# A transformer layer with gathered experts on one core: attention of chunks 3 to 7 split in two stages by head group, expert rows fetched in pairs from pick 80

## What is computed

```python
h = x + W_out [ gnorm(MLA group) ; gnorm(dilated-window group) ]
h = h + MemoryCrossAttn(rmsnorm(h), rmsnorm(mem))
h = h + PEER(rmsnorm(h))
out = rmsnorm(h)

def chunk(xc):                        # PEER, 128 tokens at a time
    q = (xc @ w_q).reshape(C, Hh, 2, half)
    s = jnp.einsum('chpd,hpnd->chpn', q, sub_keys)
    top_s, top_i = lax.top_k(s, K)
    ...
    expert = ia * PEER_KEYS + ib
    g = jax.nn.softmax(best_s, axis=-1)
    u = u_tab[expert]
    a = jax.nn.gelu(jnp.einsum('cd,chkd->chk', xc, u), approximate=False)
    return jnp.einsum('chk,chkd->cd', g * a, v_tab[expert])
```

## Time and profile before

| | before |
|---|---|
| time of three runs | 3798.14, 3781.03, 3800.05 us (median 3798.14) |
| profiled execution | span 3789.9 us; its own time isn't given apart, the span lies between the three times |
| PE busy | 2933.6 us, 77% |
| DVE busy | 2484.4 us, 66% |
| ACT busy | 1298.0 us, 34% |
| POOL busy | 1420.4 us, 37% |
| DMA | 1297.10 MB, mean 342 GB/s |

### The profile page before, as it was taken

The page is one execution under the profiler, slowest core; times in us unless marked ns, Lnnn a source line. Parts: engine busy times, 40 slices in busy tenths (PEclk is TensorE's granted clock), DMA queues, the critical chain, the costliest instruction groups (busy, mean ns, idle before and its releaser), DMA issues.

```text
span 3789.9 us, 34958 instructions
## 1 busy us (share of the span) xinstructions
PE 2933.6 (77%) x8920; PEld 1517.5 (40%) x8920; DVE 2484.4 (66%) x5699; ACT 1298.0 (34%) x3333; POOL 1420.4 (37%) x1367
## 2 busy tenths in 40 slices
PE   8797866984886598989689797787878777766665
PEld 6655533431443355555344343333333333322222
DVE  0321218786876477767437888877887887788765
ACT  1212312221121244444234544444443454344333
POOL 0000003443776376657423333333333333333332
PEclk9897888997898799999899999999989999999999
DMA  7844156777998999999889999999999999999998
GB/s 298 274 147 184 57 215 214 238 263 283 346 338 327 352 369 341 363 352 355 333 318 369 401 411 417 409 414 415 411 407 421 413 405 407 421 410 414 417 411 351
DMA packets 274454, 1297.10 MB, mean 342 GB/s; under 512 B 27888, under 2 KB 63088, under 8 KB 180464
## 3 DMA queue, kind: packets, MB, share of 16 engines
q0 software_dynamic: 195120, 1073.83, 72.2%
q1 hardware_dynamic: 74384, 203.74, 14.4%
q10 hardware_dynamic: 4752, 17.30, 1.2%
HBM read 1231.07 MB, written 63.70 MB: 342 GB/s over the span
## 4 chain that ended last, share of the span: by engine, by line
DMA 31%; issue 7%; DVE 5%; PE 4%; ACT 3%; POOL 0%; POOLq 0%; DVEq 0%; SPq 0%; ACTq 0%
DMA s_ring<-peer_uv,s_expert 17%; DMA e_more_slots<-peer_uv,s_expert 10%; PE e_acc L503 3%; DVE e_part L427 1%; PE e_product L1859 1%; DMA e_more_slots<-peer_v,s_expert 1%; DMA next_h<-e_h 1%; DMA e_h<-norm_ffn_row 1%; DMA s_scratch<-norm_final_row 1%; DVE s_ring L394 1%; ACT L341 1%; ACT s_diagonal L324 0%; ACT s_gate L343 0%; DVE s_dots L394 0%; DVE e_more_slots L394 0%
## 5 line engine op out<-in xcount | busy, mean ns | idle before, releaser
L503 PE MATMUL e_acc<-s_ring,s_diagonal 128*128 128x512 f32 (+1 forms) x2168 | 898.8, 543 | 379.6 <-ACT s_diagonal L324 352.8
L394 DVE CUSTOM_DVE_ANT_0 s_ring<-s_ring,e_x_copy 128x1024 f32<-128x1024 f32 x548 | 666.6, 1217 | 221.9 <-DMA s_ring<-peer_uv,s_expert 215.1
L503 PEld LDWEIGHTS e_acc<-s_ring,s_diagonal 128*128 128x128 f32 x2168 | 396.5, 199 | 943.5 <-ACT s_diagonal L324 587.5
L278 POOL DMA_INDIRECT s_ring<-peer_uv,s_expert x462 | 437.5, 947 | 783.1 <-DVE e_part L427 551.8
L278 POOL DMA_INDIRECT s_ring<-peer_u,s_expert x331 | 377.4, 1140 | 449.9 <-DVE s_expert L1796 230.8
L503 PE MATMUL e_acc<-e_more_slots,s_diagonal 128*128 128x512 f32 (+1 forms) x948 | 387.4, 536 | 153.9 <-ACT s_diagonal L324 146.3
L278 POOL DMA_INDIRECT s_ring<-peer_v,s_expert x325 | 373.2, 1148 | 332.0 <-PE e_acc L503 94.9
L341 ACT ACTIVATE s_dots<-s_dots 128x1 f32<-128x1 f32 x704 | 142.2, 202 | 961.3 <-DVE s_dots L394 959.0
L324 ACT ACTIVATE s_diagonal<-s_ident,s_gate 128x128 f32<-128x128 f32 x949 | 371.2, 399 | 223.0 <-PE e_acc L503 100.1
L278 POOL DMA_INDIRECT e_more_slots<-peer_uv,s_expert x231 | 217.6, 942 | 413.8 <-DVE e_part L427 273.5
L394 DVE CUSTOM_DVE_ANT_0 s_ring<-s_ring,s_x 128x1024 f32<-128x1024 f32 x245 | 299.5, 1222 | 104.6 <-DMA s_ring<-peer_u,s_expert 69.2
(11 more groups left out here) (233 smaller groups left out, 3618.5 us busy)
## 6 DMA issues: line engine op xcount, KB each, us to landing
w_in_kept<-w_in SPq DMA_DIRECT2D x8, 1104.0 KB, 11.8
w_in_gained<-w_in_kept SPq DMA_DIRECT2D x8, 1104.0 KB, 10.2
p_w_in<-w_in_gained SPq DMA_DIRECT2D x8, 1104.0 KB, 19.0
f_w_big<-w_mem_kv SPq DMA_DIRECT2D x4, 2048.0 KB, 19.2
f_w_big<-peer_w_q_t SPq DMA_DIRECT2D x2, 4096.0 KB, 17.9
peer_scores<-f_stage_s SPq DMA_DIRECT2D x16, 512.0 KB, 8.5
e_mem_scores<-mem_scores SPq DMA_DIRECT2D x2, 4096.0 KB, 14.6
e_mem_values<-mem_values SPq DMA_DIRECT2D x2, 4096.0 KB, 25.0
```

The source lines that it names most:

```text
L278: pool.indirect_dma_start(out=to, out_offset=None, in_=table, in_offset=bass.IndirectOffsetOnAxis(ap=self.expert[c % PICK_BUFFERS][:, k:k ...
L394: dve.tensor_tensor_reduce(row, row, x[:, :], 1.0, 0.0, ALU.mult, ALU.add, self.dots[:, k:k + 1]).then_inc(self.u_used, 1)
L503: last = pe.matmul(self.acc[:, at:to], self.diagonal[:, made % DIAGONALS, :], row[:, at:to], start=(n == group[0]), stop=(n == group[-1]))
```

## The change

Six things change together.

1. `PAIRS_FROM` goes from 331 to 80. u and v of a pick are gathered in one transfer from row 160 on, and u no longer leads there. `ALONE_FROM` follows, 320 to 80: from pick 80, Gelu and product are made for each pick by itself (`coeff_alone` is now `make_coeffs`).
2. The attention of chunks 3 to 7 becomes two blocks, `attend_group` for the MLA heads (rows 304 to 448) and for the dilated heads (rows 448 to 640). Units run head by head, the five chunks of a head in turn. A bias table is loaded once a head. The normalized output of both groups stays in SBUF (`mixed`), and the five output projections come after the last unit of the second block, 16 of weight each beside nb + 3 for a unit.
3. Buffers that a block doesn't need go to the ring: 6, 10, 8 and 4 slots more than 8 in the four later stages (before: none, none, 4).
4. In the attention blocks PE takes 384 columns of v, before 512.
5. DVE adds a pick's v one pick later (`add_due`), in pairs' rows of the split stages too.
6. In `project_tokens` ACT takes the stream at two more places.

A stage can also be `batched`, Gelu for four picks at once; no stage here is.

```diff
-PAIRS_FROM = 331
+PAIRS_FROM = 80
...
-    def coeff_alone(self, g):
+    def make_coeffs(self, picks):
         act = self.nc.scalar
-        c, k = divmod(g, PICKS)
-        n = g - ALONE_FROM + 1
-        if k % (2 * TOPK) == 0 or n == 1:
+        c, k = divmod(picks[0], PICKS)
+        made = picks[0] - ALONE_FROM
+        many = len(picks)
+        if k % (2 * TOPK) == 0 or made == 0:
             act.wait_ge(self.gate_ready, GROUPS * c + k // (2 * TOPK) + 1)
-        act.wait_ge(self.u_used, g + 1)
...
+        act.wait_ge(self.u_used, picks[-1] + 1)
+        act.activation(self.active[:, k:k + many], self.dots[:, k:k + many], ACT.Gelu).then_inc(self.activated_alone, many)
+        act.wait_ge(self.activated_alone, made + many)
+        for g in picks:
+            at = g % PICKS
+            act.activation(self.coeff(g), self.active[:, at:at + 1], ACT.Copy, scale=self.coeff(g)).then_inc(self.coeff_made, 1)
+        act.wait_ge(self.coeff_made, made + many)
...
+        if self.batched[self.stage_of[n]]:
+            behind = {0: [n - 8, n - 6], 1: [n - 6, n - 4]}.get(g % BATCH, [])
+            last = [n - 6, n - 4, n - 2, n]
+        else:
+            behind = [n - 2]
+            last = [n]
+        for m in behind + (last if n == end - 1 else []):
+            if m >= first:
+                add(m)
...
+                if woven:
+                    beside(stream.scalar, t, 3)
+                if more:
                     keep_x_t(t + 1)
...
+def attend_group(nc, io, group, first, end, mixed, stream, until):
...
+        UNITS = [(h, t, first + t + 1) for h in range(HEADS) for t in range(COUNT)]
...
+        weights = np.array([nb + 3 for _, _, nb in UNITS] + ([FINISH_WEIGHT] * COUNT if group == 1 else []))
+        rows_until = [begin + int(c) for c in np.floor((until - begin) * np.cumsum(weights) / weights.sum())]
...
+            stream.scalar(begin)
+            softmax(0)
+            for n, (h, t, nb) in enumerate(UNITS):
+                act.wait_ge(p_turned, n + 1)
+                act.activation(probs_t[:, n % 2, 0:P * nb], turned[:, 0:P * nb], ACT.Copy).then_inc(p_t_ready, 1)
+                stream.scalar(rows_until[n])
+                if n < LAST:
+                    softmax(n + 1)
...
+            for n, (h, t, nb) in enumerate(UNITS):
+                pe.wait_ge(exped, n + 1)
+                for k in range(nb):
+                    last = pe.transpose(turned[:, P * k:P * (k + 1)], probs[:, n % 2, P * k:P * (k + 1)], ident[:, :])
+                last.then_inc(p_turned, 1)
+                if n + 2 <= LAST:
+                    score(n + 2)
+                weigh(n)
+                stream.tensor(rows_until[n])
...
-PICK_FIRST, PROJECT_REST, ATTEND_REST = 150, 300, 640
-STAGES = [(PICK_FIRST, "pe", D), (PROJECT_REST, "split", 0), (ATTEND_REST, "split", BANK), (len(ROWS), "pe", 3 * D // 4)]
+PICK_FIRST, PROJECT_REST, ATTEND_MLA, ATTEND_REST = 150, 304, 448, 640
+STAGES = [Stage(PICK_FIRST, "pe", D), Stage(PROJECT_REST, "split", 0, 6), Stage(ATTEND_MLA, "split", 3 * P, 10),
+          Stage(ATTEND_REST, "split", 3 * P, 8), Stage(len(ROWS), "pe", 3 * D // 4, 4)]
```

More of the change, by code:

```diff
@@ L215, in __init__, with batch_at, picks_due @@
             self.loads.append(used[slot])
+    def batch_at(self, n):
+        return next(batched for (start, until, _), batched in zip(self.stages, self.batched) if start <= n < until)
+    def picks_due(self, n):
+        g = ROWS[n][1]
+        if not self.batched[self.stage_of[n]]:
+            return [g]
+        return list(range(g + 1 - BATCH, g + 1)) if g % BATCH == BATCH - 1 else []
     def mode(self, n):
@@ L1154, in _, with attend @@
                 stream.tensor(until)
-def attend(nc, io, keep, first, end, ident=None, stream=None, until=0):
+def attend(nc, io, keep, first, end):
     with ExitStack() as ctx:
@@ L1195, in attend @@
         heads_out = ps("a_heads_out", [P, WIDTH])
-        if stream is not None:
-            stream.acc = ps("a_acc", [P, BANK])
-            start = stream.at["vector"]
-            weights = np.array([nb + 3 + (PROJECT_BLOCKS if i > 0 and u == PROJECT_AT else 0) for i, u, nb in ALL_UNITS])
-            HEAD_ROWS, TAIL = 8, 8
-            begin = start + HEAD_ROWS
-            rows_until = [begin + int(c) for c in np.floor((until - TAIL - begin) * np.cumsum(weights) / weights.sum())]
         w_loaded = sem("a_w_loaded")
@@ L1307, in _ @@
             act.wait_ge(eps_set, 1)
-            if stream is not None:
-                stream.scalar(begin)
             softmax(0)
@@ L1404, in _ @@
         def _(pool):
-            if stream is not None:
-                stream.gpsimd(stream.ahead(until))
-                return
             pool.wait_ge(gain_loaded, 16)
@@ L1440, in weigh @@
                 pe.wait_ge(p_t_ready, n + 1)
-                if stream is not None and n == 0:
-                    pe.wait_ge(keep_loaded["values"], 16)
                 if u in (0, HEADS):
@@ L1497, in _ @@
                     weigh(n)
-                    project(t - 1, (rows_until[n - 1], rows_until[n]) if stream is not None else (0, 0))
+                    project(t - 1)
                 if n + 2 < len(ALL_UNITS):
```

428 lines of the change are left out of this document (322 added, 106 removed).

## The result

The changed kernel takes 3955.40 us, median of four runs (3953.85 to 3960.31); the kernel before takes 3792.59 us beside it (3781.03 to 3800.05). The ratio is 1.0438, 95% interval 1.0415 to 1.0460: slower by 4.4%. The profiled execution took 3953.91 us with a span of 3952.1. I had said 3905, within 3815 to 3965, and slower with a chance of 0.80: the time lies in the range, 9.6 us from its upper end.

What follows compares the result with a forecast made beforehand. ACT's cycle in the attention units was taken as the bound (chance 0.78). Attention +108, projection +5 and last stage -3 gave +110 us: 3900 on the 3789.9 span, 3908 on the median; said 3905, range 3815 to 3965.

Steps and rivals of the forecast that it cites:

- Direction and mechanism: Attention units: ACT's cycle of copy, Gelu's table, picks, Exp's table and Exp sets the pace; slower, chance 0.80.
- The dearer switch: Rival for ACT's table switches: a drain makes each 2.66 us, not 1.30, an estimated 185 us more; chance 0.02.
- two starts: Start of each attention block, before its units run: 28 us each, 56 together, bounds 15 and 50 each.
- the units: 80 attention units, one head of one chunk each: 6.97 us in the first half, 7.12 in the second, 564 together.
- end of the first block: Ten norms and squares, a flush and a barrier closing the first attention half: 10 us.
- projections and tail: Five output projections alone behind the units, 100 us (bounds 90 and 110), and a tail of 8 us.
- idle while PE transposes: ACT's idle time in each attention unit: 0.74 us at 512 keys, 1.18 at 1024, mean 0.96.
- The second way: Cross-check of the attention: 264 us of added ACT work against 177 us of absorbable idle time, 87 more than fits.
- DMA's pace: Rival, projection and attention: ACT's slack suffices and wider gathers pay, up to 179 us faster; chance 0.12.
- Projection: Projection stage: ACT's late squares and roots cost 5.4 us a chunk, DVE's row waits go; +5 us, bounds -15 and +30.
- Last stage: Stage that ends the kernel: 22 single rows at its start become 11 pairs, same bytes to fetch; -3 us.

Runs made afterwards that it cites:

- e1: Changed kernel with one unused Sqrt, of another table, ahead of Exp in every attention unit: 4077.48 us, ratio 1.0731.
- e3: Changed kernel with Copy in place of Gelu in the two attention blocks, so nearly no table switches (output leaves out those Gelus): 3757.27 us, ratio 0.9881.
- e5: Changed kernel with one Gelu for four picks in the two attention blocks, pairs kept: 3843.16 us, ratio 1.0091.
- e9: Changed kernel with eight useless transposes of the identity added on PE in each attention unit: 3936.22 us, ratio 1.0384.
- e8: Changed kernel with the extra slots of the two attention blocks cut from 10 and 8 to 2 and 2: 3955.83 us, ratio 1.0376.
- e6: Changed kernel with the next unit's Exp (ACT) and transposes (PE) put ahead of the picks, all table loads kept in the code: 3863.07 us, ratio 1.0139.
- e2: Changed kernel with picks taken only in every second attention unit, twice as many at once: 3996.72 us, ratio 1.0521.
- e4: Changed kernel with double rows from pick 331 again, so one Gelu for 16 picks before; split attention and extra slots kept: 3794.65 us, ratio 0.9964.

## Why the prediction was right, and where it was off

*Direction and mechanism.* Right. Between two copies stand two table loads and the picks, with 1.18 us idle. Adding loads (e1) and taking them away (e3, e5) give nearly the same price: 111.2 us for 114.7 of added work, 1.25 us for each of 165, 1.30 us for each of 88. Each of these three has something else in it (the clock, the next bound, the shared Gelus), so the price is about the load's own length, and no closer than that.

*The dearer switch.* It did not come. The Trainium skill ("ScalarE: Activation LUTs", section "What ACT_TABLE_LOAD costs") has a drain of about 1380 ns beside each load. No trace here shows it: in the timeline above the load of 1297.72 ends at 1299.00 and Exp starts at 1299.02, e1 adds 77 loads and loses no more than the added work, and e3 gets 1.25 us back for each switch.

*The size.* I said +108 us for the attention, and it is +166.0. That the total is still inside my range is in part luck: the range had bounds for the starts, the projections and the projection stage and none for the unit, and the unit is where most of the difference lies. The terms against the copies' timeline of the changed kernel:

| term | said | measured | how |
|---|---|---|---|
| two starts | 56 | 71.2 | 36.9 (to 1271.44) and 34.3 (to 1609.56) |
| the units | 564 | 596.0 | 287.0 to the 40th copy at 1558.41, 309.0 to the one at 1918.57 |
| end of the first block | 10 | 16.9 | 1558.41 to 1575.3 |
| projections and tail | 108 | 111.7 | 1918.57 to 2030.3 |
| sum | 738 | 795.8 | |

The mis-sized term is the unit: 6.97 and 7.12 us from copy to copy, measured 7.36 and 7.92 (287.0 and 309.0 over 39 steps each; the last unit is in the row that follows). For the 78 steps that makes 46.5 us. The waits of ACT close this sum. It stood idle for the transposes for 107.0 us, where 0.96 a step makes 74.9: 32.1 us. It waited for dots for 8.5 us and for DVE at the end of a chunk for 3.5, which I had put at nothing: 12.0 us. Its own work, with the small gaps between instructions, is 2.4 us more than I had. So the step that was off is "idle while PE transposes", taken from two units in which PE was on time. Where PE was on time, as in the unit above (from the load at 1294.59 to the copy's end at 1302.46, 7.87 us at 1024 keys with two picks), it holds: 1.30 for the load, 1.84 for the picks, 1.30, Exp 1.15 less 0.10 of overlap, 0.19 for the read, 1.18 idle and 1.02 for the copy are 7.88. What the sum left out:

- **The clock.** I took PE's times from a stretch at 0.93. With PE waiting for Exp in most units, the blocks had 0.83. The unit ahead of the one shown took 9.31 us (copies at 1284.35 and 1293.66), with the same number of picks, 2:

```profile
1293.66 0.92 ACT L1647 ACTIVATE g_probs_t_g<-g_turned_g 128x896 f32<-128x896 f32 x1 [2.92 <-PE g_turned_g L1792]
```

and PE in it, against the same four matmuls of two picks a unit later:

```profile
1289.97 2.87 PE L560 MATMUL g_acc_g<-g_more_slots_g,s_diagonal 128*128 128x384 f32 x4
1292.64 0.98 PE L1792 MATMUL g_turned_g<-s_ident,g_probs_g 128*128 128x128 f32 x7
...
1296.90 0.91 PE L560 MATMUL g_acc_g<-g_more_slots_g,s_diagonal 128*128 128x384 f32 x2 [0.50 <-ACT s_diagonal L355]
1297.76 0.91 PE L560 MATMUL g_acc_g<-s_ring,s_diagonal 128*128 128x384 f32 x2
```

  2.87 us for four against 0.91 + 0.91. The granted clock was 0.50 from 1284 to 1290 and 0.66 from 1290 to 1294, and 1.00 in the 8 us behind. PE, late with the picks, came late to the transposes, and ACT waited 2.92 us for them, not 0.96. Sixteen of the 78 steps took over 8.5 us. e9, whose edit adds nothing but the filling on PE, got 23.1 us of the units back with the higher clock, and 24.9 us of waits for the transposes, where the excess of these was 32.1.

- **The end of a chunk of picks.** Its sums go out through DVE and ACT's own queue, and Exp stands behind them. It made the longest step of all, 15.18 us:

```profile
1737.58 1.28 ACT L373 ACT_TABLE_LOAD   x1 [3.54 <-DVE s_scratch L538]
...
1743.58 0.20 ACT L373 ACTIVATE s_dots<-s_dots 128x1 f32<-128x1 f32 x1 [3.75 <-DVE s_dots L428]
```

  That is some 7 us above the mean step; its two waits, 3.54 and 3.75 us, are part of the 12.0 us.

*The second way*, 264 us of work less 177 of slack, gave +87, with a second start some 115, and came no nearer: it took all of ACT's idle time but 77 us as free to use, and 155.4 us stayed idle ahead of the copies.

*Starts.* 35.6 us each in place of 28, within my bounds; PE waits for the block's own q for 24.3 and 20.3 us in the waits above. Most of the difference is the wide prefetch beside these first loads: with 2 slots more than 8 (e8) they are 30.6 and 26.8 us.

*DMA's pace.* I gave 0.12 to a gain of up to 179 us. Without Gelu's switches (e3) the pairs bring 25.3 us at most. My bound had put the last stage's 412 GB/s on whole stages; e3's blocks reached 359 and 342, their starts and output projections included, and 391 in the units of the first, at a share of 1.00.

*Projection.* +5 said, +1.3 measured. DVE's waits for rows have gone from the middle of the stage, and in place of them it waits for ACT's squares and roots, 9.7 us in 180, less than the 5.4 us a chunk I had counted (waits of DVE from 1030 to 1210):

```profile
DVE p_x_stat L1053 <- ACT p_x_stat L993: 5.3, 3, 3.2
...
DVE p_c_stat L1065 <- ACT p_c_stat L1010: 4.4, 3, 2.2
```

*Last stage.* -3 said, -2.5 measured, which is less than this stage scatters in the table.

## What to carry to other kernels

On an engine that holds one table of functions at a time, count the switches in each turn of the innermost cycle before you split a batched function into single ones: here two switches of 1.3 us in each of 80 units cost 206 us, eight times the 25 us at most that the wider gathers brought. Put work that the next engine waits for (Exp, ahead of the transposes) first in the queue, and work that only has to be done some time behind it; that gave 97 us back where ACT was the bound, and 8 at most where it wasn't. And an engine's idle time isn't slack while it stands inside a cycle: ask what would run in it, and whether the thing it waits for would come later too.

## What the runs showed of the hardware that I had not expected

Waits for another engine cost TensorE more than their own length here, as its granted clock fell beside them. In the changed kernel's blocks PE was busy 71 and 80% of the time (240.62 of 340.80, 361.92 of 455.00) and had a clock of 0.83; single stretches stood near the lower level of 1.2 GHz:

```profile
1294.00:1302.00 8.00, 5.71 (x30) 3.55 (x29) 4.58 (x8) 6.63 (x12) 2.96 (x3) 1.00 0.88 302
1302.00:1316.00 14.00, 10.33 (x48) 6.86 (x47) 8.30 (x15) 11.50 (x21) 2.92 (x3) 0.90 0.84 298
1316.00:1324.00 8.00, 8.00 (x24) 5.41 (x23) 4.98 (x8) 5.20 (x11) 1.54 (x2) 0.53 0.24 98
```

The first is at 1.00, 2.4 GHz; the last, in the same loop, at 0.53, with PE busy in all of its 8 us. Ahead of it PE had been busy for 5.71 of 8 and 10.33 of 14 us. In the units of the first block PE's waits for Exp came to 47.4 us in 35 in the changed kernel; in e1 they were 71.5 us in 35, and that block had 0.70. In e6 there was one, of 0.8 us, and the block had 0.92, though PE then waited 41.5 us for diagonals. e2 had 0.75 in both blocks with shorter waits for Exp (20.5 us in 18), so the length of these waits isn't the whole of it. Eight useless transposes a unit raised the clock from 0.83 to 0.93 and took 23.7 us off the attention.

Gathers of rows of 8 KB (u and v together) ran at 403 GB/s at a DMA share of 0.99 in the last stage and at 359 at 0.94 in e3's first block, where those of 4 KB ran at 344 at 0.97 in e4's. These windows count all transfers, and e3's stretch was also the shorter one, so what the width of a row is worth by itself isn't shown: the kernel before, with 4 KB rows, had 350 at 0.94.
